# Gate projections in 1024-column groups with seven block products, and strip transfers issued by GpSimd

## What is computed

```
xn = rmsnorm(x)
rq, rk, rv, rz, dq, dk, dv, dz, g_ret, g_diff = split(xn @ w_in)
o_ret  = rmsnorm(retention(rot(rq), rot(rk), rv)) * silu(rz)
o_diff = rmsnorm(diff_attention(rot(dq), rot(dk), dv, lam)) * 0.8 * silu(dz)
mixed  = sigmoid(g_ret) * (o_ret @ w_ret_up) + sigmoid(g_diff) * (o_diff @ w_diff_up)
out    = rmsnorm(x + mixed @ w_out)
```

## Time and profile before

| | us |
|---|---|
| median of 3 runs | 1091.44 (1089.77 to 1091.87) |
| the profiled execution | 1090.99 |
| its span | 1089.1 |
| PE busy | 1077.8 (99%) |
| DVE busy | 744.9 (68%) |
| ACT busy | 543.0 (50%) |
| POOL busy | 36.4 (3%) |
| DMA queue of SP, share of 16 engines | 67.8% |

### The profile page before, as it was taken

One profiled execution on the slowest core, in us unless ns is written; L12 is line 12 of the kernel. 1 busy time (PEld: TensorE's weight loads), 2 busy tenths in 40 slices (PEclk: granted clock), 3 DMA queues, 4 the chain that ended last, 5 costly groups with the idle time before them and its releaser, 6 DMA issues.

```text
span 1089.1 us, 13206 instructions
## 1 busy us (share of the span) xinstructions
PE 1077.8 (99%) x4864; PEld 897.1 (82%) x4864; DVE 744.9 (68%) x924; ACT 543.0 (50%) x701; POOL 36.4 (3%) x57
## 2 busy tenths in 40 slices
PE   9999999999999999999999999999999999999997
PEld 8888888888888888888888888888888888888785
DVE  6685575485567688866766776676757675677796
ACT  6554455344455544444653465446444654444454
POOL 0100000000000000000100001000200020000000
PEclk9999999999999999999999999999999999999999
DMA  9877667666666565767576757676676667676743
GB/s 330 302 246 223 177 198 208 195 196 211 193 187 198 187 224 169 226 197 231 170 210 193 229 176 207 204 209 192 201 219 203 205 189 250 218 244 202 257 162 135
DMA packets 133985, 227.98 MB, mean 209 GB/s; under 512 B 14496, under 2 KB 40864, under 8 KB 133408
## 3 DMA queue, kind: packets, MB, share of 16 engines
q1 hardware_dynamic: 133632, 226.86, 67.8%
q10 hardware_dynamic: 288, 0.27, 0.1%
HBM read 210.84 MB, written 2.10 MB: 196 GB/s over the span
## 4 chain that ended last, share of the span: by engine, by line
PE 95%; DVE 2%; issue 1%; DMA 1%; ACT 1%; SPq 0%; DVEq 0%; POOL 0%; POOLq 0%; ACTq 0%
PE bank L1565 26%; PE bank L1567 26%; PE bank L1566 26%; PE bank L1572 4%; PE bank L1573 4%; PE bank L1574 4%; PE bank L1642 1%; PE bank L1641 1%; PE bank L1640 1%; DVE w_lo L1068 0%; DMA raw<-w_out_dram 0%; PE bank L1537 0%; SPq L511 0%; PE bank L1541 0%; PE bank L1520 0%
## 5 line engine op out<-in xcount | busy, mean ns | idle before, releaser
L1068 DVE TENSOR_TENSOR w_lo<-raw,w_hi 128x1024 fp32r<-128x1024 f32 x364 | 449.3, 1240 | 300.3 <-ACT w_hi L714 299.9
L714 ACT ACTIVATE w_hi<-raw 128x1024 fp32r<-128x1024 f32 x364 | 385.4, 1060 | 464.9 <-PE bank L1567 398.7
L1565 PE MATMUL bank<-w_hi,xt_hi 128*128 128x512 f32 x1136 | 443.8, 391 | 0.0
L1567 PE MATMUL bank<-w_hi,xt_lo 128*128 128x512 f32 x1136 | 442.6, 390 | 0.0
L1566 PE MATMUL bank<-w_lo,xt_hi 128*128 128x512 f32 x1136 | 442.5, 390 | 0.0
L1567 PEld LDWEIGHTS bank<-w_hi,xt_lo 128*128 128x128 f32 x1136 | 213.4, 188 | 44.5
L1565 PEld LDWEIGHTS bank<-w_hi,xt_hi 128*128 128x128 f32 x1136 | 213.4, 188 | 43.7 <-DVE w_lo L1068 0.2
L1566 PEld LDWEIGHTS bank<-w_lo,xt_hi 128*128 128x128 f32 x1136 | 213.4, 188 | 43.5
L1567 PE MATMUL bank<-w_hi,ot_lo 128*128 128x512 f32 x128 | 49.9, 389 | 0.0
L1565 PE MATMUL bank<-w_hi,ot_hi 128*128 128x512 f32 x128 | 49.8, 389 | 0.0
L1566 PE MATMUL bank<-w_lo,ot_hi 128*128 128x512 f32 x128 | 49.8, 389 | 0.0
(11 more groups left out here) (184 smaller groups left out, 855.1 us busy)
## 6 DMA issues: line engine op xcount, KB each, us to landing
raw<-w_in_dram SPq DMA_DIRECT2D x284, 512.0 KB, 4.2
raw<-w_ret_up_dram SPq DMA_DIRECT2D x32, 512.0 KB, 4.6
raw<-w_diff_up_dram SPq DMA_DIRECT2D x32, 512.0 KB, 4.9
raw<-w_out_dram SPq DMA_DIRECT2D x32, 512.0 KB, 4.6
rot<-squares_t SPq DMA_DIRECT2D x96, 64.0 KB, 2.4
zs<-squares_t SPq DMA_DIRECT2D x48, 64.0 KB, 2.2
normed<-squares_t SPq DMA_DIRECT2D x48, 64.0 KB, 2.2
raw<-w_in_dram SPq DMA_DIRECT2D x8, 256.0 KB, 5.5
```

What stands on the lines that cost most here:

```text
L714: act.activation(w_hi[:, s, :, :], raw[:, s, :, :], ACT.Copy).then_inc(hi_ready, 1)
L1068: dve.tensor_tensor(w_lo[:, s, :, :], raw[:, s, :, :], w_hi[:, s, :, :].bitcast(F32), ALU.subtract) \
L1565: pe.matmul(bank[bk][:, :], hi, w_hi[:, s, kk, :], start=k == 0, stop=False)
L1567: return pe.matmul(bank[bk][:, :], lo, w_hi[:, s, kk, :], start=False, stop=k == KT - 1)
```

## The change

1. The eight gate groups of 512 columns leave the iterations. They become two new paired phases of two 1024-column groups each, `RET_GATE` behind the retention iterations (now 6 groups each) and `DIFF_GATE` behind the diff iterations (now 4 groups each). The gates are no longer read from banks straight into a sigmoid: shared parts are joined, own parts added (`gate_own`, DVE), and `gates` (ACT) takes the sigmoid.
2. The end of the last iteration now runs inside the first gate group. `small_products` puts `weights_by_v` after the unit k = 2 of that group.
3. All strip DMAs are issued by POOL, in order with its `head_rstd` and the multiplication of `zs`.
4. In `out`, x is put into the own banks of the first group too (`x_to_banks`, ACT, at the last step ahead of `out`), and `add_x` on DVE goes.
5. Some steps move: q is rotated at step 13 in both retention iterations (was 13 and 10) and at 10 in diff iterations (was 8); the second heads of a retention iteration come one step earlier; `read_mt` is at 8(j+1)+5 and 42 (was +4 and 41).

```diff
-RET_ITS, RET_G = 2, 8
-DIFF_ITS, DIFF_G = 4, 5
+RET_ITS, RET_G = 2, 6
+DIFF_ITS, DIFF_G = 4, 4
-PAIRED = (U_UP, U_OUT)
+PAIRED = (U_RET_GATE, U_UP, U_DIFF_GATE, U_OUT)
-    own, shared = (4, 5, 6, 7), (0, 1, 2, 3)
-    return (own, shared) if group % 2 == 0 else (shared, own)
+    lower, upper = (4, 5, 0, 1), (2, 3, 6, 7)
+    return (lower, upper) if group in (0, 2, 4, 7) else (upper, lower)
...
 # in gpsimd, no longer in sync
+            def turn(slot, event, dst, size):
+                pool.wait_ge(squares_ready[slot], event + 1)
+                for i in range(STRIPS):
+                    rows = slice(i * SQUARE, (i + 1) * SQUARE)
+                    pool.dma_start(dst[:, i, :], squares_t[rows, slot, 0:STRIPS * size].rearrange("c (j e) -> c j e", j=STRIPS)) \
+                      .then_inc(turned[slot], 16)
...
             def round_sums(group, u):
+                if group in (first_group(RET_GATE), first_group(DIFF_GATE)) and u == SEVEN_AT[0]:
+                    for b in range(BLOCKS):
+                        act.wait_ge(filled[6 + b], (ret_high(RET_ITS, 0) if group == 0 else diff_high(DIFF_ITS, 0)))
...
+            def gates(group):
+                dst = mixed if phase_of(group) == RET_GATE else gate
+                for i in range(SUMS):
+                    b, j = pair_blocks(group)[i]
+                    act.wait_ge(own_drained, SUMS * group + i + 1)
+                    act.activation(dst[:, b, j * COLS:(j + 1) * COLS], shared_part(group, i), ACT.Sigmoid,
+                                   scale=x_rstd[:, b:b + 1]).then_inc(gates_ready, 1)
...
+                if q == U_OUT - 1:
+                    act.wait_ge(own_drained, SUMS * first_group(OUT))
+                    x_to_banks(first_group(OUT))
...
+            def own_free(group):
+                own = pair_banks(group)[0]
...
+                elif phase_of(group) == OUT:
+                    pe.wait_ge(x_in_banks, SUMS * (group - first_group(OUT) + 1))
...
+            def shared_free(group, late):
+                shared = pair_banks(group)[1]
+                if group in (first_group(RET_GATE), first_group(DIFF_GATE)):
+                    low, high = (ret_low(RET_ITS, 0), ret_high(RET_ITS, 0)) if group == first_group(RET_GATE) \
+                        else (diff_kv(DIFF_ITS, 0), diff_high(DIFF_ITS, 0))
+                    for bk in shared[2:] if late else shared[:2]:
+                        pe.wait_ge(drained[bk], high if late else low)
...
                     pair_unit(n0 + k, k, own, t_hi, t_lo)
+                    small_products(n0 + k)
                     if k % KU == 0 and k // KU - 1 in SEVEN_AT:
+                        if k // KU - 1 == SEVEN_AT[0]:
+                            shared_free(group, True)
                         seven_by_sums(group, k - KU, own, shared, t_hi, t_lo)
```

More of the change, by code:

```diff
@@ L443, in weight_sums @@
         def weight_sums(group):
[L445 to L448, removed]
+            first = (group % PAIR_GROUPS) * PAIR_COLS
+            return (mixed[:, :, PAIR_COLS:], zs[:, :, :], gate[:, :, PAIR_COLS:], mixed[:, :, first:first + PAIR_COLS])[phase_of(group)]
         def weight_sum(group, i):
@@ L737, in read_keys_hi @@
                 act.activation(dst, src, ACT.Copy).then_inc(keys_hi_ready, 1)
-            def sigmoid_gate(n_last, banks, dst, col):
-                group_done(n_last)
-                for b in range(BLOCKS):
-                    act.activation(dst[:, b, col:col + COLS], bank[banks + b][:, :], ACT.Sigmoid,
-                                   scale=x_rstd[:, b:b + 1]) \
-                       .then_inc(drained[banks + b], 1)
             def squares(m, fills):
@@ L971, in _ @@
-                if out_s in (KT + 2, KT + 3, KT + 4, KT + 5):
-                    square_h(out_s - (KT + 2))
+                for phase in range(len(PAIRED)):
+                    for p in range(PAIR_GROUPS):
+                        s = q - PAIRED[phase] - p * KT
+                        if s == KT - AHEAD:
+                            copy_first(first_group(phase) + p)
+                        if phase in (RET_GATE, DIFF_GATE) and s == KT + 1:
+                            gates(first_group(phase) + p)
@@ new lines, in lambda_whole, with gate_own @@
+            def lambda_whole():
+                dve.wait_ge(lam_step, 2)
+                dve.scalar_tensor_tensor(out=neg_lam[:, :], in0=lam_exp[:, 1:2], scalar=-LAM_INIT, in1=lam_exp[:, 0:1],
+                                         op0=ALU.add, op1=ALU.subtract).then_inc(neg_lam_ready, 1)
+            def gate_own(group, i):
+                part = shared_part(group, i)
+                own_full(dve, group, i)
+                dve.wait_ge(shared_drained, group + 1)
+                dve.tensor_tensor(part, part, bank[pair_banks(group)[0][i]][:, :], ALU.add).then_inc(own_drained, 1)
@@ L1471, in add_square @@
+                if q - U_OUT - KT in (4, 5):
+                    for i in range(2):
+                        weigh(2 * (q - U_OUT - KT - 4) + i)
             def add_square(b, slot, src, dst, step):
@@ L1726, in pair_group, with paired_phase @@
                 pair_last(n0 + KT - by_bank, by_bank, own, t_hi, t_lo)
-            for group in range(PAIR_GROUPS):
-                pair_group(group, ot_hi, ot_lo, ot_lo_ready, HEADS)
+            def paired_phase(phase, t_hi, t_lo, ready, count):
+                for group in range(first_group(phase), first_group(phase) + PAIR_GROUPS):
+                    pair_group(group, t_hi, t_lo, ready, count)
+            for it in range(RET_ITS):
+                n0 = U_RET + it * RET_UNITS
+                for s in range(RET_UNITS):
+                    g, u = unit_at(s) if it == 0 else (s // UNITS, s % UNITS)
+                    banks = 4 if it == 0 and g == 2 else 2 * (g % 2)
+                    if u == 0:
+                        start_group(banks, 1 if banks == 4 else ret_low(it, g // 2))
+                    unit(n0 + s, u, banks, xt_hi, xt_lo)
+                    small_products(n0 + s)
```

941 lines of the change are left out of this document (475 added, 466 removed).

## The result

| | before | after |
|---|---|---|
| median, us | 1090.69 (1089.77 to 1091.87, 4 runs) | 1113.99 (1109.00 to 1117.34, 4 runs) |
| ratio | 1 | 1.0209, 95% interval 1.0169 to 1.0250 |
| profiled execution, its span | 1090.99, 1089.1 | 1117.34, 1115.2 |
| last matmul starts at | 1080.99 | 1103.67 |
| from there to the end of the span | 8.1 | 11.5 |

The change makes the kernel 2.1% slower. (The kernel before has one execution more here than in the table ahead of the prediction.) The profiled execution is the slowest of the four (the others: clock 0.989 to 0.994, this one 0.986), so sums of its trace come out 3.3 us above the median.

A forecast was written before the change was run, and what follows sets the result against it. PE, busy 99% of the span, was taken as the bound. Terms of -5.4 for matmuls and waits summed to +7.9 us, with +3.4 for the clock +11.3, on 1090.99: 1102.3 us, range 1093 to 1115.

The forecast's parts named there:

- expensive issues: Rival, chance 0.17: POOL's strip issues cost 1.5 us each, delaying `out`, k = 12 and four diff iterations; 1115 us.
- Matmuls removed: Four groups of 1024 columns, two places each, 24 matmuls become 21: 24 fewer on PE's path, -5.4 us.
- First wait: Start of each gate phase: `weights_by_v` waits for a later `read_v_lo` on DVE; +2.1 us retention, +2.9 us diff.
- I cost the iterations at nothing: Strips from POOL inside the iterations: readers stand 10.9 us behind the squares, so no cost at 1.1 us an issue.
- the argument against contention: Against POOL's DMAs stalling beside DVE: DVE's time goes to two-source operations, 1240 ns for 1024 elements, showing no two-port mode.
- Second wait: Gate phases, end of unit k = 6: PE waits for banks 6 and 7; +2.1 us in each of two phases.
- The start of `out`: First matmul of `out` waits for ACT's four bank copies, behind late strips and token sums; +3.7 us.
- k = 12: In `out`: the old 2.47 us wait stays and grows because `read_mt` comes one unit later; +0.4 us.
- The clock: Drops after the waits of 2.9 and 3.7 us, +3.4 us; three of 2.1 us uncounted, 5.1 in the range.
- waits inside the diff iterations: Sign that would show the forecast wrong, as would PE's waits totalling under 6 us.
- The estimate of 3.0 us: Start of `out`: 3.0 instead of 3.7 us, from the skill's 1 us to first byte for GpSimd, 0.6 for SyncE.
- The faster rival: Rival, chance 0.12: DVE and ACT end in time, so the gate phases' four waits vanish; 1087.7 us with cheap issues.

The follow-up runs named there:

- e5: Changed kernel with `read_v_lo` of the last iteration one step earlier on DVE in both phases, ahead of `rest_of_seven`; 1107.39 us, ratio 1.0142.
- e2: Changed kernel with the strip transfers issued by SP again, between the weight loads as before; 1105.87 us, ratio 1.0127.
- e4: Changed kernel with the exponential of lambda moved from the first step of `ret_up` to ahead of the diff phase's first exponential; 1111.23 us, ratio 1.0174.
- e3: Changed kernel with the four copies of x into banks four units earlier on ACT; 1109.61 us, ratio 1.0154.
- e1: Kernel before with only the strip transfers moved to POOL; 1093.98 us, ratio 1.0021.
- e9: Kernel before plus 216 dummy copies of 1 KB issued by POOL between the retention and diff phases, strips still on SP; ratio 1.0026.
- e7: Changed kernel with e2 to e6 together, plus `sum_weights` of the first gate groups behind `read_v_lo`; 1088.64 us, ratio 0.9971.
- e12: As e7, with the last tail group's strips issued ahead of a weight load and read earlier, ahead of the sums, for k = 12; 1084.41 us, ratio 0.9934.
- e8: Kernel before with one early DMA, the decay table's 1 MB load, issued by POOL instead of SP; ratio 1.0010.
- e10: Kernel before with one late DMA, the 1 MB of final norm weights, issued by POOL behind about 1022 us; ratio 1.0005.
- e6: As e5, with squares and both `norm_head` ahead of `round_sums` and `rest_of_sums` in the first gate groups; 1102.98 us, ratio 1.0104.
- e11: As e7, but with the strips issued by POOL as in the changed kernel; 1093.79 us, ratio 1.0015.

## Why the prediction was right, and where not

1102.3 us was forecast, within 1093 to 1115, slower with 0.82; the median is 1113.99. The kind of result and its mechanism were right, the size 11.7 us short: +11.3 us were forecast, and +23.3 measured. That the median lies in the range is partly luck. The upper bound of 1115 stands for expensive issues, which did not happen, and one of the four executions took 1117.34.

- **Matmuls removed**: 24, -5.4 us, right by the count (4864 to 4840) and by the account of the result, which closes to 0.4 us with it.
- **First wait**: 2.1 and 2.9 forecast, 2.14 and 4.93 measured. The working for retention was exact, and e5 confirms what it rests on. The step that failed in the diff phase is the one that takes the slot of k = 5 as free for its load at the old time: 1.4 of the 2.0 us missing there are the `w_lo` of 3.77 us beside POOL's product and the later load behind it (e2), that is, POOL's strips. The other 0.6 us are in e2 too (3.53 against 2.9) and were not traced to one row. "I cost the iterations at nothing" looked at the readers of the strips alone, and the argument against contention ("two-source operations ... shows no such mode") took the rule of the Trainium skill (SBUF — State Buffer, section "Who interferes with whom") on one-source operations for the whole of that section; the two-source operation is the one that was blocked.
- **Second wait**: 2.1 in each phase, 2.08 and 1.20 measured. In the diff phase it is 1.79 without a low clock ahead of it (e5) and 1.20 with the costliest one (the changed kernel, e2, e4), so the two terms seem not to be independent.
- **The start of `out`**: 3.7 forecast, 2.66 measured; e3 shows the cause. POOL's issue was taken at 1.1 us and is 0.54, but the last strip lands about 4.4 us after the end of its issue (1000.90 to 1005.35), not 1.6. Together the strips have landed 8.8 us behind the first issue instead of 10.2, which takes 1.4 from the term; 0.3 come back, since PE was ready that much sooner. The rest of the working was right: from there to the rounding of the token sums it is 5.1 us again (1005.35 to 1010.47), and the copies follow at once (rows below).
- **k = 12**: +0.4 forecast, 2.87 against 2.47 measured.
- These terms are 13.3 us forecast, 13.4 measured. That is luck: +2.0 in the first wait against -0.9 and -1.0 in the second and at the start of `out`.
- **The clock** is the term that was mis-sized: "+3.4" for two waits, "I count nothing" for the three of 2.1 us. In the profiled execution all three waits of about 2 us dropped it, and so did the three longer ones: 12.2 us in six drops, 10.3 more than before, against 3.4 forecast. The range had 5.1 for the waits of 2.1 us, but not that the one of 4.93 would cost 3.0.
- **Not foreseen**: 1.88 us at `ret_up` behind the lambda exponential (e4), 0.54 and 0.89 us of small waits, and 3.4 us behind the last matmul (e1, e9). The prediction has no term behind the last matmul.
- A sign to be wrong by, "waits inside the diff iterations", did show once, with 0.54 us; e2 and e7, with SP's strips, have no such wait.
- **Slips in the working**, small and without weight: eight issues of 1.1 and 1.6 us from 978.1 end at 988.5, not 988.3; 11.8 less 9.6 is 2.2, not 2.1; and the cover in the iterations, 10.9 us for eight issues and a landing, is gone above 1.2 us an issue, not 1.3. The estimate of 3.0 us takes a time to the first byte for the time between two issues, so it says nothing of this term.

The rival of expensive issues gave 1115, the nearest number, by a mechanism that is not there: an issue is cheap. The faster rival, no waits at the starts of the phases, is what e7 and e12 had to make by hand.

The strips of tail group 2, POOL's issues and then ACT, against the earlier trace rows:

```profile
996.57 4.33 POOL L633 DMA_DIRECT2D rot<-squares_t  x8 [18.04 <-DVE squares_t L1137]
...
1005.35 1.15 ACT L945 ACTIVATE xt_hi<-rot 128x512 fp32r<-128x512 f32 x2 [1.82 <-DMA rot<-squares_t]
...
1010.47 0.63 ACT L743 ACTIVATE right_hi<-normed 128x512 fp32r<-128x512 f32 x1 [1.50 <-DVE normed L1084]
1011.01 2.14 ACT L963 ACTIVATE bank<-gate 128x512 f32<-128x512 f32 x4
```

And the median landing of the strips, from the DMA issues (KB each, us):

```profile
rot<-squares_t POOLq DMA_DIRECT2D x96, 64.0 KB, 3.7
zs<-squares_t POOLq DMA_DIRECT2D x48, 64.0 KB, 3.8
normed<-squares_t POOLq DMA_DIRECT2D x48, 64.0 KB, 3.6
zs<-squares_t POOLq DMA_DIRECT2D x32, 48.0 KB, 3.0
```

From SP the same strips take 2.4, 2.2, 2.2 and 2.0 us (the kernel before). The Trainium skill (DMA: Bandwidth & Descriptors, section "Latency and other measured facts") gives about 1 us to the first byte for a DMA issued by GpSimd and 0.6 for one by SyncE, 0.4 apart. From issue to landing these rows are 1.0 to 1.6 us apart, 1.3 in the first.

## What to carry to other kernels

Merging work into fewer matmuls pays on a bound PE only after the seams between phases have been timed: an operation listed ahead of another on DVE or ACT there costs its own length and often a slow clock behind it, here some 25 us for the 5.4 of the matmuls. Each of the long waits at the phase starts went away by reordering a few operations, with no added work; small ones of 0.4 and 0.5 us came in their place, and the gain that was left is 0.3% (e7). Before DMAs are moved to GpSimd, price three things: their later landing, what its other operations do to DVE when they shift, and the end of the program.

## What was not expected of the hardware

**The clock after a wait.** Waits of PE of 1.2 us or more behind its start, over the 14 profiled executions, by length and by whether the matmuls behind ran slow (granted clock 0.50):

| wait, us | clock fell | did not |
|---|---|---|
| 1.20 to 1.79 | 0 | 9 |
| 1.84 to 2.14 | 8 | 5 |
| 2.37 to 4.93 | 19 | 3 |

The same wait in the same place goes both ways: 2.14 us at `weights_by_v` dropped it in the changed kernel and in e3 and e4, and not in e2, whose window behind it reads:

```profile
289.50:291.50 2.00, 2.00 (x19) 2.00 (x19) 1.38 (x2) 0.00 (x0) 0.00 (x0) 1.00 0.90 330
```

In the changed kernel a drop cost 1.7 to 3.0 us, 2.0 on average; the six waits themselves are 2.8 on average. With three waits of 1.88 to 2.14 us this is also the likely reason for the wide spread of its four runs (1109.0 to 1117.3, granted clocks 0.994 to 0.986), against 2.1 us before; it was not tested by itself.

**GpSimd beside DVE.** One `w_lo` took 3.77 us instead of 1.23 while POOL multiplied, and by how the two operations met the loss was DVE's alone or was shared (e2). The longest `w_lo` is 2.3 us in all seven versions with SP's strips (the kernel before, e2, e7, e8, e9, e10, e12), and 3.7 to 3.8 in all seven with POOL's (the changed kernel, e1, e3, e4, e5, e6, e11).

**GpSimd's DMA queue.** 0.54 us an issue (SP: 0.64), landing 1.0 to 1.6 us later than SP's, and a DRAIN of POOL at the end of the program of 9.1 to 9.8 us after some 220 issues, against 0.7 without, of which 2.7 to 3.7 us lengthened the program.
